# Neighbourhood attention on one core: steps taken in pairs, scores with the opposite sign

## The reference, cut to what matters

```
s_loc = q . k_window * scale + bias          # 8 rows x 16 columns around the query
s_ctx = q . k_ctx * scale                    # 256 context positions
p     = softmax(concat(s_loc, s_ctx))
out   = p_loc . v_window + p_ctx . v_ctx
```

## Time and profile before

| | us |
|---|---|
| median of three runs | 1766.1 (1761.38 to 1766.35) |
| the profiled execution | 1766.19 |
| its span, first to last instruction | 1764.5 |
| mean granted TensorE clock | 0.982 of full |

### The profile page before, as it was taken

How to read it: one execution, slowest core, us unless ns; L and a number is a source line. 1 busy time by engine, 2 the same in 40 slices (tenths; PEclk the granted TensorE clock), 3 DMA queues, 4 the chain that set the end, 5 groups by cost and what they waited for, 6 DMA issues and landing times.

```text
span 1764.5 us, 23045 instructions
## 1 busy us (share of the span) xinstructions
PE 1712.2 (97%) x9114; PEld 1447.1 (82%) x9114; DVE 978.7 (55%) x1367; ACT 710.6 (40%) x1042; POOL 148.2 (8%) x199
## 2 busy tenths in 40 slices
PE   7999999999999999999999999989999899999998
PEld 7888888889898788888878888877778688888887
DVE  4346554666455666566677454248885555435543
ACT  4244343335344556555553323126663333213320
POOL 3000000000000000000000000036661000000000
PEclk8999999999999999999999999969999899999999
DMA  8311223324234443665442122311101233343322
GB/s 264 97 49 48 72 72 119 121 96 143 73 112 128 120 136 121 189 186 182 156 140 85 48 72 72 126 68 37 37 24 51 69 95 88 98 113 93 89 82 81
DMA packets 227591, 178.64 MB, mean 101 GB/s; under 512 B 5971, under 2 KB 217278, under 8 KB 227502
## 3 DMA queue, kind: packets, MB, share of 16 engines
q1 hardware_dynamic: 218206, 142.74, 27.2%
q0 software_dynamic: 8576, 32.23, 5.5%
q10 hardware_dynamic: 720, 2.41, 0.4%
HBM read 171.37 MB, written 9.13 MB: 102 GB/s over the span
## 4 chain that ended last, share of the span: by engine, by line
PE 86%; DVE 5%; ACT 4%; issue 2%; POOL 2%; DMA 0%; DVEq 0%; ACTq 0%; POOLq 0%
PE ps L1575 27%; PE ps L1577 26%; PE ps L1576 26%; POOL sc L2136 2%; DVE w_lo L974 1%; ACT w_hi L564 1%; PE ps L1705 1%; PE ps L2019 1%; PE ps L1944 1%; ACT mod_tmp L687 1%; PE ps L2049 1%; PE ps L1644 1%; ACT vt_h L907 1%; PE ps L1966 0%; PE ps L1691 0%
## 5 line engine op out<-in xcount | busy, mean ns | idle before, releaser
L1575 PE MATMUL ps<-h_hi,w_hi 128*128 128x512 f32 x1024 | 404.4, 395 | 4.7 <-DVE h_lo L1386 2.5
L1576 PE MATMUL ps<-h_lo,w_hi 128*128 128x512 f32 x1024 | 401.1, 392 | 0.0
L1577 PE MATMUL ps<-h_hi,w_lo 128*128 128x512 f32 x1024 | 401.0, 392 | 0.0
L974 DVE TENSOR_TENSOR w_lo<-w_raw,w_hi 128x2048 fp32r<-128x2048 f32 (+1 forms) x136 | 290.2, 2134 | 128.6 <-ACT w_hi L564 128.5
L564 ACT ACTIVATE w_hi<-w_raw 128x2048 fp32r<-128x2048 f32 (+1 forms) x136 | 242.5, 1783 | 177.1 <-PE ps L1577 151.5
L1575 PEld LDWEIGHTS ps<-h_hi,w_hi 128*128 128x128 f32 x1024 | 193.7, 189 | 45.1 <-DVE w_lo L974 3.2
L1577 PEld LDWEIGHTS ps<-h_hi,w_lo 128*128 128x128 f32 x1024 | 193.6, 189 | 41.2
L1576 PEld LDWEIGHTS ps<-h_lo,w_hi 128*128 128x128 f32 x1024 | 193.8, 189 | 38.8
L1575 PE MATMUL ps<-xg_hi,w_hi 128*128 128x512 f32 x352 | 139.5, 396 | 2.4 <-DVE w_lo L974 2.4
L1577 PE MATMUL ps<-xg_hi,w_lo 128*128 128x512 f32 x352 | 137.3, 390 | 0.0
L1576 PE MATMUL ps<-a_lo,w_hi 128*128 128x512 f32 x352 | 137.1, 389 | 0.0
(11 more groups left out here) (323 smaller groups left out, 3018.4 us busy)
## 6 DMA issues: line engine op xcount, KB each, us to landing
mod_raw<-in_l_w_mod POOLq DMA_DIRECT2D x24, 1024.0 KB, 7.9
w_raw<-in_w_ffn_in SPq DMA_DIRECT2D x44, 512.0 KB, 5.0
w_raw<-in_l_ffn_w_up SPq DMA_DIRECT2D x44, 512.0 KB, 4.6
w_raw<-in_w_in SPq DMA_DIRECT2D x40, 512.0 KB, 5.0
w_raw<-in_l_na_w_qkv SPq DMA_DIRECT2D x24, 512.0 KB, 4.6
w_raw<-in_w_mem_kv SPq DMA_DIRECT2D x16, 512.0 KB, 4.0
w_raw<-in_w_ffn_out SPq DMA_DIRECT2D x16, 384.0 KB, 3.6
w_raw<-in_l_ffn_w_down SPq DMA_DIRECT2D x16, 384.0 KB, 3.6
```

The source lines that it names most:

```text
L974: v.tensor_tensor(wlo[s][:, 0:size], raw[s][:, 0:size], whi[s][:, 0:size].bitcast(F32), ALU.subtract).then_inc(w_lo, 1)
L1575: mm(o, w_h, x_h, start=first, stop=False, **kw)
L1576: mm(o, w_h, x_l, start=False, stop=False, **kw)
L1577: return mm(o, w_l, x_h, start=False, stop=last, **kw)
```

## The change

It does five things. The steps go in pairs, on PE, ACT and DVE. The scores are made with the opposite sign (the gain of q, the bias and the window mask change theirs), so that the smallest one is the negated maximum that the exponential needs, and the exponential takes scale -1. The [128 x 1] instruction of the maximum goes: the bias instruction starts from the reduction's result, for which it now waits. The lead-in makes four maxima, four exponentials and three reciprocals. DVE's loop over the pairs is written out. The lists of one round, g even, are then:

```diff
-                act.activation(sc[:, tau, :], bank(tau), ACT.Exp, bias=na_nmax[:, tau:tau + 1],
+                act.activation(sc[:, tau, :], bank(tau), ACT.Exp, bias=na_nmax[:, tau:tau + 1], scale=-1.0,
...
-                for st in range(8):
+                for st in range(0, 8, 2):
                     g = 8 * a + st
-                    if not (last and st + 2 >= 8):
-                        na_exp(g + 2, (st + 2) % 4)
-                    act.wait_ge(np_ps, g + 1)
-                    act.activation(np_hi[:, st % 2, :], bank(4 + st % 2), ACT.Copy).then_inc(np_h, 1)
                     if st % 4 == 0 and not (first and st == 0):
                         na_out(a if st else a - 1, 0 if st else 1, 2 * a + (1 if st else 0))
+                    for m in range(2):
+                        act.wait_ge(np_ps, g + (m + 1))
+                        act.activation(np_hi[:, m, :], bank(4 + m), ACT.Copy).then_inc(np_h, 1)
+                    for m in range(2):
+                        if not (last and st + 4 >= 8):
+                            na_exp(g + (4 + m), (st + m) % 4)
...
+                    if not (last and st + 3 >= 8):
+                        na_den_step(g + 3, (st + 3) % 4)
...
+                    for m in range(2):
+                        dve.wait_ge(np_h, g + (m + 1))
+                        low(np_lo[:, m, :], bank(4 + m), np_hi[:, m, :]).then_inc(np_l, 1)
+                    if not (last and st + 4 >= 8):
+                        for m in range(2):
+                            na_max_step_in(a, st + 4 + m, (st // 4 + 1) % 2)
+                        na_den_step(g + 4, st % 4)
...
-                v.tensor_reduce(na_nmax_c[:, tau:tau + 1], ps[:, tau, 256:512], AX.X, ALU.max, negate=True)
+                v.tensor_reduce(na_nmax_c[:, tau:tau + 1], ps[:, tau, 256:512], AX.X, ALU.min).then_inc(ns_red, 1)
+                dve.wait_ge(ns_red, g + 1)
                 v.tensor_tensor_reduce(out=ps[:, tau, 0:256], in0=ps[:, tau, 0:256],
                                        in1=bias[b][:, (0, 1, 1, 2)[tau], :, :].rearrange("p i j -> p (i j)"),
-                                       scale=1.0, scalar=-3.0e38, op0=ALU.add, op1=ALU.max,
-                                       accum_out=na_max[:, tau:tau + 1]).then_inc(ns_red, 1)
-                dve.wait_ge(ns_red, g + 1)
-                v.scalar_tensor_tensor(na_nmax[:, tau:tau + 1], na_max[:, tau:tau + 1], -1.0, na_nmax_c[:, tau:tau + 1],
-                                       ALU.mult, ALU.min).then_inc(ns_max, 1)
+                                       scale=1.0, scalar=na_nmax_c[:, tau:tau + 1], op0=ALU.add, op1=ALU.min,
+                                       accum_out=na_nmax[:, tau:tau + 1]).then_inc(ns_max, 1)
...
-            for g in range(4 * NA_HEADS):
+            for g in range(0, 4 * NA_HEADS, 2):
+                a, st = divmod(g, 8)
                 na_transpose(g)
+                na_transpose(g + 1)
+                if st and a + 1 < NA_HEADS // 2:
+                    na_v(a + 1, st // 2 - 1)
                 if g + 4 < 4 * NA_HEADS:
                     na_scores(g + 4)
-                if g:
-                    na_values(g - 1)
-                a, st = divmod(g, 8)
-                if st in NA_V_STEPS and a + 1 < NA_HEADS // 2:
-                    na_v(a + 1, NA_V_STEPS.index(st))
-            na_values(4 * NA_HEADS - 1)
+                    na_scores(g + 5)
+                na_values(g)
+                na_values(g + 1)
...
-                r = pool.tensor_tensor(bias[head % 2][:, kind, :, :], gb[head % 2][:, :, x0:x0 + 32], w, ALU.add)
+                r = pool.tensor_tensor(bias[head % 2][:, kind, :, :], w, gb[head % 2][:, :, x0:x0 + 32], ALU.subtract)
```

More of the change, by code:

```diff
@@ L111, in constants @@
         key = min(max(16 * strip - 8, 0), 32) + jl
-        c[:, C_WIN + 32 * n:C_WIN + 32 * n + 32] = np.where((key >= start) & (key < start + WIN_W), 0.0, NEG)
+        c[:, C_WIN + 32 * n:C_WIN + 32 * n + 32] = np.where((key >= start) & (key < start + WIN_W), 0.0, -NEG)
     return c
@@ L240, in program @@
         eps_sq = small[:, 184:185]
-        na_nmax_c, na_max, na_nmax = (small[:, x:x + 4] for x in (164, 168, 172))
+        na_nmax_c, na_nmax = (small[:, x:x + 4] for x in (164, 172))
         na_den, na_rden = small[:, 176:180], small[:, 180:184]
@@ L371, in head_jobs @@
             return []
-        NA_V_STEPS = (3, 5, 6)
         span = [0, 8, 24, 32]
@@ L916, in na_pair @@
             def na_pair(a, buf, first=False, last=False):
-                for st in range(8):
+                for st in range(0, 8, 2):
                     g = 8 * a + st
-                    if not (last and st + 2 >= 8):
-                        na_exp(g + 2, (st + 2) % 4)
-                    act.wait_ge(np_ps, g + 1)
-                    act.activation(np_hi[:, st % 2, :], bank(4 + st % 2), ACT.Copy).then_inc(np_h, 1)
                     if st % 4 == 0 and not (first and st == 0):
                         na_out(a if st else a - 1, 0 if st else 1, 2 * a + (1 if st else 0))
-                    if st in NA_V_STEPS and not last:
-                        r = NA_V_STEPS.index(st)
+                    for m in range(2):
[4 more added lines that the diff above has]
+                            na_exp(g + (4 + m), (st + m) % 4)
+                    if st and not last:
+                        r = st // 2 - 1
                         na_v(1 - buf, r, 3 * (a + 1) + r + 1)
             act.preload_act_table(ACT.Exp)
-            na_exp(0, 0)
-            na_exp(1, 1)
+            for g in range(4):
+                na_exp(g, g)
             for r in range(3):
@@ L1155, in mod_vectors @@
                 v.tensor_tensor(modv[:, 0:48], bank(5)[:, 0:48], vecB[:, V_BMOD:V_BMOD + 48], ALU.add).then_inc(mod_sb, 1)
-                v.tensor_scalar(qgain, vcol(V_QG), NA_DIM ** -0.5, None, ALU.mult).then_inc(mod_sb, 1)
+                v.tensor_scalar(qgain, vcol(V_QG), -NA_DIM ** -0.5, None, ALU.mult).then_inc(mod_sb, 1)
                 dve.wait_ge(mod_sb, 3)
@@ L1486, in na_pair @@
             def na_pair(a, buf, first=False, last=False):
-                for st in range(8):
+                for st in range(0, 8, 2):
                     g = 8 * a + st
-                    if not (last and st + 1 >= 8):
-                        na_den_step(g + 1, (st + 1) % 4)
                     if not (last and st + 3 >= 8):
[L1492 to L1495, removed]
+                        na_den_step(g + 3, (st + 3) % 4)
                     if st % 4 == 0 and not (first and st == 0):
                         na_out(a if st else a - 1, 0 if st else 1, 2 * a + (1 if st else 0))
-                    if st in NA_V_STEPS and not last:
-                        r = NA_V_STEPS.index(st)
+                    for m in range(2):
[5 more added lines that the diff above has]
+                        na_den_step(g + 4, st % 4)
+                    if st and not last:
+                        r = st // 2 - 1
                         na_v(1 - buf, r, 3 * (a + 1) + r + 1)
@@ L1506, in na_max_step_in @@
                     dve.wait_ge(bias_done, 2 * a + st // 4 + 1)
-                v.tensor_reduce(na_nmax_c[:, tau:tau + 1], ps[:, tau, 256:512], AX.X, ALU.max, negate=True)
+                v.tensor_reduce(na_nmax_c[:, tau:tau + 1], ps[:, tau, 256:512], AX.X, ALU.min).then_inc(ns_red, 1)
+                dve.wait_ge(ns_red, g + 1)
                 v.tensor_tensor_reduce(out=ps[:, tau, 0:256], in0=ps[:, tau, 0:256],
                                        in1=bias[b][:, (0, 1, 1, 2)[tau], :, :].rearrange("p i j -> p (i j)"),
-                                       scale=1.0, scalar=-3.0e38, op0=ALU.add, op1=ALU.max,
-                                       accum_out=na_max[:, tau:tau + 1]).then_inc(ns_red, 1)
-                dve.wait_ge(ns_red, g + 1)
-                v.scalar_tensor_tensor(na_nmax[:, tau:tau + 1], na_max[:, tau:tau + 1], -1.0, na_nmax_c[:, tau:tau + 1],
-                                       ALU.mult, ALU.min).then_inc(ns_max, 1)
-            for st in range(3):
+                                       scale=1.0, scalar=na_nmax_c[:, tau:tau + 1], op0=ALU.add, op1=ALU.min,
+                                       accum_out=na_nmax[:, tau:tau + 1]).then_inc(ns_max, 1)
+            for st in range(4):
                 na_max_step_in(0, st, 0)
-            na_den_step(0, 0)
+            for g in range(3):
+                na_den_step(g, g)
             dve.wait_ge(vp_in[0], 16)
@@ L1525, in _ @@
             na_pair(0, 0, first=True)
-            with dve.Fori(1, 7, 2) as a:
+            for a in range(1, 7, 2):
                 na_pair(a, 1)
```

## The result

The changed kernel took 1775.6 us in the median of ten runs (1770.23 to 1780.83), the kernel before 1766.1 beside it (1761.38 to 1774.05). The ratio is 1.0052, with a 95% interval of 1.0032 to 1.0072: **slower by 0.5%**. The forecast had been 1765.2, so the sign was wrong; the time lies at the upper end of the range, and what happened is rival C. The profiled execution took 1779.09 (span 1777.4). Of its 12.9 us over the one before, 4.1 were lost ahead of the stage (v_out's last copy ends at 1158.38, before at 1154.24), where PE runs the same list with its clock at 0.91 instead of 0.97 from 948 to 1048. In the traces of this document that copy ends anywhere between 1154.11 and 1163.98, though all of these kernels do the same work ahead of it. So I compare **lengths of the stage**, from the end of that copy to the first matmul behind the stage: 182.64 before, 191.88 after, 9.2 longer.

A forecast was written before the change was run, and what follows sets the result against it. PE was busy 97% of the span, with 1.8 us of stalls in a 20.83 us pair; DVE and ACT's serial chain would set the new pair. +2.0 - 0.6 - 2.0 - 0.3 = -0.9 us gave 1765.2, range 1752 to 1776.

The forecast's parts named there:

- rival C: Slower: the clock falls at PE's 1.7 us pause at round 4's na_v; 6 us a fall, 1771 to 1783; chance 0.14.
- from there to step 8: First transposes to step 8's: 25.6 us instead of 26.2, -0.6, with 15.6 us of work at half clock.
- six pairs: Middle of the neighbourhood stage: a pair of heads takes 20.50 us against 20.83, -2.0 over six.
- last pair: Last pair of heads, which has no na_v: 17.3 us instead of 17.56, -0.3.
- Part 3: The new loop over pairs of heads: DVE and ACT's serial chain sets the rounds; 20.50 us a pair against 20.83.
- The walk: Stepping through the new lists for a whole pair of heads, PE's waits at na_v included: 20.50 us.
- the ring: Serial chain of lows, maxima, exponential and high on DVE and ACT: 4.37 us a round where PE needs 4.15.
- Part 1: PE's order: two steps share the changes of block, saving 0.33 a round; PE needs 17.8 us a pair of heads.
- Part 2: DVE's maximum step: the sign instruction goes, the bias instruction waits for the reduction; 0.87 us instead of 1.14.
- Rival D: Slower: the bias instruction with its scalar from memory waits for POOL; +1 to +2 a pair, 1772 to 1777; chance 0.10.
- Rival B: DVE and ACT's serial chain is hidden and PE sets the pair at 17.8: 1749, half of it 1757; chance 0.24.
- Part 4: Both ends of the stage: +2.0 until the first transposes, -0.6 to step 8, -0.3 at the end.

The follow-up runs named there:

- v_behind_values: The changed kernel with na_v moved on PE from ahead of the scores to behind the values: 1763.92 us, 0.9991 of the kernel before.
- pause_filled: The changed kernel with four transposes of round 4's second step made four times over in PE's pause, 12 more matmuls a pair: 1767.27 us.
- sign_only: The kernel before with only the negated scores and new maximum step, DVE's loop written out, no steps in pairs: 1764.41 us, 0.9988 of the kernel before.

## Why the prediction was wrong

| term | forecast | measured |
|---|---|---|
| to the first transposes | +2.0 | +1.65 |
| from there to step 8 | -0.6 | -2.0 |
| six pairs | -2.0 | +8.27 |
| last pair | -0.3 | +1.34 |
| sum | -0.9 | +9.24 |

**The step that failed** is in Part 3: "PE stands 1.7 us in round 4 and 1.0 in round 6, with the scores queued behind it". The pause of round 4 was foreseen in place and size (1.80 to 1.82), but its cost was taken as the time of standing alone, with the clock left at full. The runs show the reverse: standing in round 4 costs nothing, standing in round 6 0.27 a pair, and the clock behind the pauses 1.27. The fall of the clock was put into rival C with a chance of 0.14. The rows I had the earlier trace rows spoke neither way: a pause of 2.35 had held the clock, one of 2.00 had not. I let the stalls of up to 0.5 us in the stage decide, which are no evidence for 1.7. Without the clock's 1.27 a pair of 22.20 would have been 20.93, as good as no change.

**Rival C was right in mechanism and wrong in price**, twice over: it counted one to three falls where seven came, and 6 us for each where a pair with one is 1.3 longer in the mean. The 17 us at half clock were read off the lead-in the earlier trace rows; the falls in the pairs last 6.8 or 3.4 us. And a PE at half speed first uses up its own waits: in those windows it is busy for all 4.00 us, where with the clock held (*v_behind_values*) it waits 17.2 of 120. The Trainium skill, "TensorE: Matmul & The Clock Gate", section "HAM oscillation — how this bites in real kernels", tells of a kernel that falls to half clock in every wait between its bursts. The trace agrees that a fall comes in each pair from the second on, but the clock was back long before the pair was over, and the 1832 us of the prediction are far off.

**The walk** of the ring (Part 3) had 20.50 for a pair; with the clock held the same order of lists has at most 20.93 (*pause_filled*, with its 12 matmuls). So the walk was at most 0.4 too small. The forecast's upper end had named the handings for that; which term it was is not shown. That the ring, and not PE, sets the pair was right: opening it took 1.8 us a pair.

**Part 1** was right: two transposes stand in one row of eight matmuls with no change of block (1.06 from start to end), and with the ring open a pair comes to 18.84, 1.0 above the 17.8 that PE needs by this count; 0.6 of that are waits at the values (3.7 us in 108). **Part 2** was right for the new step and wrong for what it replaces. Timeline of DVE, one step of 0.86:

```profile
1206.42 0.49 DVE L1512 CUSTOM_DVE_ANT_0 ps<-ps,bias,small 128x256 f32<-128x256 f32 x1
1206.83 0.14 DVE L1512 DVE_READ_ACCUMULATOR2_ANT small<- 128x1 f32 x1
1206.83 0.42 DVE L1510 TENSOR_REDUCE small<-ps 128x1 f32<-128x256 f32 x1
1207.28 0.49 DVE L1512 CUSTOM_DVE_ANT_0 ps<-ps,bias,small 128x256 f32<-128x256 f32 x1
```

Of the 0.27 that it was to save a step the old order shows 0.22 (*sign_only*), where POOL's normalisation fell on the old instruction; in the new order it is 0.05. **Rival D** did not occur. Shortest, median and longest of the 51 in the middle of the stage:

```profile
L1512 DVE CUSTOM_DVE_ANT_0 ps<-ps,bias,small x51: 491/493/495, 1202.0 to 1339.9; 128x256 f32<-128x256 f32 x51
```

The instruction is 0.08 longer than in the earlier trace rows, and it is so with POOL at work and without: 492 to 493 ns in the six of the 51 that run beside POOL, 491 to 495 in the others. **Rival B** came true only with another order of ACT and DVE: the objection, that their lists are fixed and the ring serial, was right.

**Part 4**: the first transposes came within 0.35 of the forecast, and their lateness has the cause given there: the four copies, 2.57 us long, run beside POOL's normalisations. From there to step 8 it went 1.4 better than forecast. The half clock at the stage's start ended 10 us behind the first transposes (1184; before, 17 us, 1185), where the forecast had 15.6 us of work at it; how much of the 1.4 is due to that was not measured. The last pair went 1.6 worse. It has a fall too, behind the longest wait at the values, and by the timeline PE waits 3.8 us in it where it waited 2.1 before:

```profile
1343.97 0.27 PE L1577 MATMUL ps<-np_hi,vt_h 128*64 128x128 f32 x1 [2.43 <-DVE np_lo L984]
```

This wait stands in the first round that has no scores left for PE; the forecast of 17.3 did not name it.

## What to carry to other kernels

A pause of TensorE has two prices, the time and the clock behind it. Where a reordering puts a wait of about a us or more ahead of queued matmuls, look for another place for the waiting instruction (here behind the values: 1.55 us a pair) before counting its cost. And when two edits both relieve the same contention, price the second one in the order that the first one leaves: taking the sign instruction away shortened a step by 0.22 us alone and by 0.05 beside the pairs, and was worth 1.0 us a pair again once the ring was open. When a ring runs through two engines, each loop-carried result needs other work between its end and its use; putting one exponential off by a round was worth 1.8 us a pair.

## What was not expected of the hardware

- In the stage the clock fell behind pauses of 0.8 and 1.41 us and did not behind five of 1.50 and one of 1.99, nor behind one of 2.35 in the middle of the kernel.
- The falls in the changed kernel's pairs lasted 6.8 and 3.4 us in turn, and a pair with one was 1.9 to 2.2 and 0.4 to 0.5 longer.
- The same four copies on DVE took 2.57 us beside POOL's normalisations and 0.90 ahead of them; a [128 x 1] instruction took 0.16 with POOL idle, 0.38 beside its work, and up to 0.73.
- The bias instruction with a scalar from memory takes 0.493 us, with a constant 0.409 to 0.424 (51 in the kernel before).
